# A fused two-block transformer kernel on one core: the loading order and closing norm of the second expert layer, and the order of three steps in the rwkv pair loop

## What is computed

```python
def rwkv_readout(y, q, p):            # first block, each head of 64 columns
    mean = jnp.mean(y, axis=-1, keepdims=True)
    var = jnp.mean(jnp.square(y - mean), axis=-1, keepdims=True)
    yn = ((y - mean) * lax.rsqrt(var + RW_GN_EPS)).reshape(b_, n, RW_DIM) * ln_w + ln_b
    bonus = jnp.einsum('blhn,bldhn,hn->blh', r, k, rk)[..., None] * v
    return (yn + bonus.reshape(b_, n, RW_DIM)) * g

# second block, for every group and expert in it
hg = jnp.einsum('td,edf->tef', xf, w_gate[gi]); hu = jnp.einsum('td,edf->tef', xf, w_up[gi])
act = jax.nn.silu(hg) * hu * comb[:, gi, :, None]
out = out + jnp.einsum('tef,efd->td', act, w_down[gi])
h = h + gate_f * out
return _rms_norm(h, norm_out_w)       # the kernel's result
```

## Time and profile before

| | us |
|---|---|
| median of 3 runs (3620.74 to 3626.2) | 3621.44 |
| the profiled execution | 3619.01 |
| its span in the trace | 3617.2 |
| PE busy, share of the span | 3184.0, 88% |
| DVE busy | 1488.0, 41% |
| ACT busy | 988.5, 27% |
| `route`, from its first transfer to the first instruction of the experts | 3243.97 to 3278.62 |
| experts, to the last down product | 3278.62 to 3581.0 |
| stores, gathers, sums, last norm | 3581.0 to 3617.2 |

### The profile page before, as it was taken

One profiled execution on the slowest core, in us unless ns is written; L12 is line 12 of the kernel. 1 busy time (PEld: TensorE's weight loads), 2 busy tenths in 40 slices (PEclk: granted clock), 3 DMA queues, 4 the chain that ended last, 5 costly groups with the idle time before them and its releaser, 6 DMA issues. The chain is left out here.

```text
span 3617.2 us, 54475 instructions
## 1 busy us (share of the span) xinstructions
PE 3184.0 (88%) x23420; PEld 1762.2 (49%) x23420; DVE 1488.0 (41%) x3058; ACT 988.5 (27%) x1956; POOL 46.7 (1%) x65
## 2 busy tenths in 40 slices
PE   7899999998799999789995987787989999884995
PEld 3566666666655555444442332334455554441432
DVE  3677776877457568510023110103242424331122
ACT  2344344334124655510011000002324243310000
POOL 0000000000000000000000000000000000000001
PEclk9999999999799999889997999998999999986998
DMA  4122222211311222243056999963111011037998
GB/s 174 54 67 65 80 69 83 77 59 50 111 51 64 79 80 69 102 151 116 0 204 281 421 421 421 421 274 157 73 47 73 27 69 47 7 139 295 417 417 328
DMA packets 119456, 555.31 MB, mean 154 GB/s; under 512 B 32320, under 2 KB 35120, under 8 KB 83632
## 3 DMA queue, kind: packets, MB, share of 16 engines
q1 hardware_dynamic: 113072, 532.95, 38.4%
q0 software_dynamic: 3456, 12.58, 0.9%
q10 hardware_dynamic: 2688, 6.29, 0.4%
HBM read 518.03 MB, written 33.74 MB: 153 GB/s over the span
## 5 line engine op out<-in xcount | busy, mean ns | idle before, releaser
L2347 PE MATMUL mh_ps<-mh_w_ahead,xmT 128*128 128x512 f32 x768 | 336.5, 593 | 0.0
L2082 PE MATMUL ex_ps<-ex_ring,ex_xs 128*64 128x512 f32 x896 | 244.9, 636 | 49.8 <-DMA ex_ring<-expert_slabs_in 37.5
L495 PE MATMUL rw_ps<-hT,rw_w 128*128 128x512 f32 (+1 forms) x640 | 255.8, 529 | 7.8 <-PEq L63 5.8
L2347 PEld LDWEIGHTS mh_ps<-mh_w_ahead,xmT 128*128 128x128 f32 x768 | 144.7, 190 | 167.1 <-issue 165.2
L2082 PEld LDWEIGHTS ex_ps<-ex_ring,ex_xs 128*64 128x64 f32 x896 | 82.7, 146 | 201.9 <-issue 199.9
L1273 PE MATMUL sg_ps<-hTp,sg_w 128*128 128x512 f32 x384 | 170.8, 598 | 0.0
L495 PEld LDWEIGHTS rw_ps<-hT,rw_w 128*128 128x128 f32 x640 | 112.1, 191 | 92.4 <-issue 82.8
L2331 PE MATMUL mh_ps<-xmT,mh_w_ahead 128*128 128x512 f32 x256 | 125.0, 622 | 14.8 <-PEq L63 8.5
L2166 DVE TENSOR_TENSOR ex_hid<-ex_hid,ex_ps 128x512 f32<-128x512 f32 x16 | 11.0, 688 | 284.9 <-PE ex_ps L2082 284.9
L1797 PE MATMUL se_ps<-se_w,se_mT 128*128 128x512 f32 x256 | 114.8, 606 | 6.5 <-DMA se_w<-w_out_in 6.5
L2974 PE MATMUL ge_ps<-ge_ring,ge_xs 128*64 128x512 f32 x512 | 116.0, 607 | 2.7 <-DVE ge_xsq L3069 2.7
(11 more groups left out here) (602 smaller groups left out, 5315.1 us busy)
## 6 DMA issues: line engine op xcount, KB each, us to landing
ex_ring<-expert_slabs_in SPq DMA_DIRECT2D x148, 1024.0 KB, 26.8
ge_ring<-expert_slabs_in SPq DMA_DIRECT2D x52, 2048.0 KB, 11.9
mh_w_ahead<-head_slabs_in SPq DMA_DIRECT2D x16, 2048.0 KB, 7.9
rw_mod_w<-mod_w_in SPq DMA_DIRECT2D x64, 384.0 KB, 4.1
ex_first<-expert_slabs_in SPq DMA_DIRECT2D x22, 1024.0 KB, 26.3
rw_mod_w<-ada_in SPq DMA_DIRECT2D x64, 256.0 KB, 3.3
sg_kern<-cum_dram SPq DMA_DIRECT2D x64, 256.0 KB, 3.2
ex_ring<-expert_slabs_in SPq DMA_DIRECT2D x7, 2048.0 KB, 13.8
```

The source lines that it names most:

```text
L495: mm = pe.matmul(where[j, part], w[:, k, P * j:P * j + P], tokens, start=k == 0, stop=k == KC - 1)
L2082: mm = pe.matmul(ps[halves[j], bank, :], src[:, k, halves[j]], home(g + j)[0][:, k, :], start=k == 0, stop=k == KC - 1)
L2347: mm = pe.matmul(ps[:, 4 + t, :], xmT[:, k, P * t:P * t + P], w[:, slot, k, :], start=k == 0, stop=k == KC - 1)
```

## The change

In the rwkv loop: banks 0 and 1 of `near` are swapped, and `near` has one more wait; the bonus product moves ahead of `turn_y`, and so does the first of the three dense steps, which waits for one group of `near` fewer; on ACT `keep_mid(c, 1)` moves ahead of `deviation(c - 1)`. In the second block: `settle` keeps x in SBUF and stores none, and loads the gate and norm rows; `route` loads two slabs and no x; `grouped_experts` loads slabs 2 to 5 of the first pair itself, starts the first gate product one turn earlier, loads two slabs again at the end and not four, lets SP store half of the last quarter rows, and computes and stores the last norm tile by tile, with a root on one element to load ACT's table ahead. `last_residual` is gone.

```diff
-        NEAR = (2, 1, 0)
+        NEAR = (2, 0, 1)
 ...
                 def near(c, d):
                     pe.wait_ge(s.filled, 2 * c + d + 1)
+                    if c:
+                        pe.wait_ge(state_ready[1], 10 * c)
 ...
                         keys(c, 0)
-                        if c:
-                            turn_y(c - 1)
                         pe.wait_ge(s.prepared, c + 1)
                         pe.matmul(ps[:, 3, :], halves, ksum[:, :], start=True, stop=True).then_inc(s.bonus_done, 1)
                     if prep:
                         if p:
                             pe.wait_ge(s.w_in, 16 * p)
                         if core:
+                            pe.wait_ge(s.near_kept, 3 * c + 2)
+                        project_part(1, 0, 0, 1)
+                    if core and c:
+                        turn_y(c - 1)
+                    if prep:
+                        if core:
                             pe.wait_ge(s.near_kept, 3 * c + 3)
-                        project_part(1, 0, 0, 3)
+                        project_part(1, 0, 1, 3)
 ...
                         keep_diag(c, 1)
+                        keep_mid(c, 1)
                         if c:
                             deviation(c - 1)
                         keep_diag(c, 2)
-                        keep_mid(c, 1)
                         keep_mid(c, 2)
 ... settle
-                for t in range(NTT):
+                for t in range(NTT if x_out is not None else 0):
                     sp.wait_ge(s.summed, H * t + H)
                     sp.dma_start(x_out[tile(t), :], x[:, t, :]).then_inc(s.x_stored, 16)
 ... route: with stage(nc, landed.all), and at SP's end
+                sp.wait_ge(landed.rows, rows)
 ... grouped_experts, SP
                     load_rows(0)
                     load_quarters(0)
-                    load_slab(0, 4)
-                    load_slab(0, 5)
+                    for n in range(2, 6):
+                        load_slab(0, n)
                     load_rows(1)
 ...
+                    sp.wait_ge(s.up_used, 2 * NP - 1)
+                    load_slab(0, 0)
+                    load_slab(0, 1)
+                    sp.wait_ge(s.yeq_kept, NP)
+                    for h in range(2):
+                        sp.dma_start(quarter_rows(NP - 1, 1, h), yeq[quarter[2 + h], :]).then_inc(s.yeq_out, 16)
+                    for t in range(NTT):
+                        sp.wait_ge(s.normed, t + 1)
+                        sp.dma_start(x_out[tile(t), :], normed(t)).then_inc(s.x_stored, 16)
+                    sp.wait_ge(s.x_stored, 16 * NTT)
 ... PE
                     turn_rows(0)
-                    turn_quarters(0)
                     for i in range(NP):
                         last = i + 1 == NP
-                        pe.wait_ge(s.xs_kept, turns_before(i + 1, i // 2 + 1))
+                        pe.wait_ge(s.xs_kept, turns_before(i + 1, i // 2 + 1) if i else 1)
 ...
-                            up_quarters(i, n)
+                            if i:
+                                up_quarters(i, n)
+                            elif n == 0:
+                                turn_quarters(0)
+                        if i == 0:
+                            pe.wait_ge(s.xs_kept, 2)
+                            up_quarters(0, 0)
+                            up_quarters(0, 1)
 ... ACT
+                    act.activation(sq[:, 0:1], cst("ones")[:, 0:1], ACT.Sqrt).then_inc(s.squared, 1)
                     for t in range(NTT):
                         act.wait_ge(s.added, t + 1)
-                        if t:
-                            act.wait_ge(s.squared, t)
+                        act.wait_ge(s.squared, t + 1)
                         act.activation(sq[:, :], x[:, t, :], ACT.Square, accum_out=ss[:, t:t + 1]).then_inc(s.squared, 1)
+                        act.wait_ge(s.mean, t + 1)
+                        act.activation(ss[:, t:t + 1], ss[:, t:t + 1], ACT.Sqrt).then_inc(s.root, 1)
 ... DVE
+                    def scale(t):
+                        dve.wait_ge(s.root, t + 1)
+                        link(dve.reciprocal(ss[:, t:t + 1], ss[:, t:t + 1]))
+                        dve.scalar_tensor_tensor(normed(t), x[:, t, :], ss[:, t:t + 1], orow, ALU.mult, ALU.mult).then_inc(s.normed, 1)
 ... behind the two sums of a tile t
                         ins.then_inc(s.added, 1)
+                        if t:
+                            scale(t - 1)
+                        dve.wait_ge(s.squared, t + 2)
+                        dve.tensor_scalar(ss[:, t:t + 1], ss[:, t:t + 1], 1.0 / D, EPS, ALU.mult, ALU.add).then_inc(s.mean, 1)
+                    scale(NTT - 1)
 ... program
+            settle(..., x2, None, ..., xn_keep=xn, x_keep=x, ahead=[gate, norm_out row, four gate pieces])
+            route(..., [(ring[:, n, :], a["expert2_slabs"][n]) for n in range(2)], (landed, 96))
-            last_residual(nc, ss[:, :], orow[:, :], x, out)
```

More of the change, by code:

```diff
@@ L1725, in _, with settle @@
                     dve.tensor_tensor(m[:, t, cols], ga_n, gb_n, ALU.add).then_inc(s.merged, 1)
-def settle(nc, cst, source, rows, norm, x_in, x_out, cols, head, lg, xT=None, xn_dram=None, xn_keep=None, ahead=()):
+def settle(nc, cst, source, rows, norm, x_in, x_out, cols, head, lg, xT=None, xn_dram=None, xn_keep=None, x_keep=None, ahead=()):
     NTT, H, KB = SEQ // P, 2, 8
@@ L1780, in _ @@
                         sp.dma_start(xn_dram[tile(t), :], xn[:, place(t), :]).then_inc(xn_stored[t % 2], 16)
-                sp.wait_ge(s.x_stored, 16 * NTT)
+                if x_out is not None:
+                    sp.wait_ge(s.x_stored, 16 * NTT)
                 if xn_dram is not None:
@@ L1973, in _ @@
                 dve.tensor_copy(lg.rearrange("p t n -> p (t n)"), ps[:, 6, 0:NL * NTT])
[L1976 to L1999, removed]
 CAP = 2 * SEQ // NE
@@ L2767, in first_of_ties, with route @@
         link(dve.tensor_tensor(hot[:, :, e], hot[:, :, e], a, ALU.is_gt))
-def route(nc, cst, raw, bias, weight, slot, npass, ahead):
+def route(nc, cst, raw, bias, weight, slot, npass, ahead, before):
     NTT, G, E = SEQ // P, 4, 4
@@ L2788, in route @@
         ps = keep.enter_context(nc.psum_tensor("rt_ps", [P, 2, 512], F32, allow_name_mangling=True))
-        with stage(nc) as (s, block, _):
+        landed, rows = before
+        with stage(nc, landed.all) as (s, block, _):
             @block.sync
@@ L2898, in grouped_experts, with quarter_rows @@
                 x_in = [s.x_in0, s.x_in1]
+                def quarter_rows(i, b, h):
+                    first = P * NP + 64 * i + 32 * b
+                    return ye_dram[first:first + 32, 512 * h:512 * h + 512]
                 ye_out = [s.ye_out0, s.ye_out1]
@@ L2918, in _ @@
                     load_quarters(0)
-                    load_slab(0, 4)
-                    load_slab(0, 5)
+                    for n in range(2, 6):
+                        load_slab(0, n)
                     load_rows(1)
-                    for i in range(NP):
-                        nxt = (i + 1) % NP
-                        if 1 <= i and i + 1 < NP:
+                    for i in range(NP - 1):
+                        if i:
                             load_rows(i + 1)
-                        if i % 2 == 1 and i + 1 < NP:
+                        if i % 2 == 1:
                             load_quarters((i + 1) // 2)
@@ L3311, in program @@
                 mixer_heads(nc, masks, xmT, tok, a["head_slabs"], a["gdn_taps"], a["ret_decay"], rope, norm_w[:, :], m, w, xe_dram[0:NE * SLOTS, :])
-            settle(nc, cst, (m, a["w_out2"], None, None), (mod2[0:1, 2 * D:3 * D], None), (col_a, col_sh), x2, x3,
-                   (a["norm_ffn"], part(mod2, 0, 4), part(mod2, 0, 3)), (a["route_w"], 20), wide(20), xn_keep=xn)
+            gate_of = lambda lo, hi, n: mod2[0:1, 5 * D + lo:5 * D + hi].broadcast_to([n, hi - lo])
+            rows = [nc.sbuf_tensor(name, shape, F32, side="right") for name, shape in (("x4", [P, 4, D]), ("gate4", [P, D]), ("gate_q", [P, 512]), ("orow4", [P, D]))]
+            x, gate, gate_q, orow = (keep.enter_context(r) for r in rows)
+            landed = Sems(nc, keep)
+            settle(nc, cst, (m, a["w_out2"], None, None), (mod2[0:1, 2 * D:3 * D], None), (col_a, col_sh), x2, None,
+                   (a["norm_ffn"], part(mod2, 0, 4), part(mod2, 0, 3)), (a["route_w"], 20), wide(20), xn_keep=xn, x_keep=x,
+                   ahead=[(gate[:, :], gate_of(0, D, P), landed.rows), (orow[:, :], a["norm_out"].broadcast_to([P, D]), landed.rows)] +
+                         [(gate_q[32 * n:32 * n + 32, :], gate_of(512 * (n % 2), 512 * (n % 2) + 512, 32), landed.rows) for n in range(4)])
         with ExitStack() as moe:
             sb = lambda name, shape: moe.enter_context(nc.sbuf_tensor(name, shape, F32))
-            x, gate, gate_q, orow, ss = sb("x4", [P, 4, D]), sb("gate4", [P, D]), sb("gate_q", [P, 512]), sb("orow4", [P, D]), sb("ss4", [P, 4])
+            ss = sb("ss4", [P, 4])
```

39 lines of the change are left out of this document (20 added, 19 removed).

## The result

The changed kernel takes 3600.86 us (median of 4 runs, 3596.62 to 3602.84), the one before 3622.8 in its 4 runs beside them: ratio 0.9943, 95% interval 0.9931 to 0.9956. It is 22 us faster; 26.9 were forecast. The time lies 6.9 us above the forecast and 0.4 above the range. Of the 6.9 us 4.9 are the gain that is missing, 1.4 come from the median of before (3622.8 and not 3621.4), and 0.5 from rounding 3594.5 to 3594. The profiled execution of after took 3600.97, its span is 3599.3.

A forecast was written before the change was run, and what follows sets the result against it. Transfers were taken to hold `route`, PE to set the experts' pace, and PE to wait for y in rwkv. Terms -18.5, -3.7, -1.8, -1.9 and -1 gave -26.9 from median 3621.4: 3594.5, stated as 3594, range 3585 to 3600.5.

The forecast's parts named there:

- Part 1: Start of the experts: with two slabs in `route` and x kept, DVE and not transfers holds the stage; -18.5 us.
- Part 2: First pair of the experts: first turn to pair 1 takes 42.0 and not 45.7 us; -3.7 us, late slabs costing zero.
- Part 3: End of the kernel: -1.8 us up to the first gather, -1.9 us from there to the end.
- Part 4: rwkv loop: bonus and dense step fill the wait for y, but root and low-rank products start later; -1 us.
- the three cases -1.9, +0.5 and +3: rwkv loop, cost over six pairs in us: clock stays up, falls as before, or falls in all.
- the clock stays up: rwkv loop: the clock does not fall, given the shorter idle times; -1.9 us over six pairs.
- falls as before: rwkv loop: the clock falls in three of the six pairs, as in the kernel before; +0.5 us.
- (b): rwkv moves cost: root's 0.74 us passed on in seven pairs, or clock falls in all; +5 us, 3600; chance 0.15.
- (a): rwkv moves give all they aim at: root not late, low-rank products do not wait; 3585; chance 0.12.
- (c): Experts' start gives half: loop entry was hidden in SP's wait, or slabs hold first pairs; 3603 to 3605; chance 0.06.
- (d): Experts: slower than before, slabs late in every pair because their lead is two; 3630; chance 0.01.
- (e): `route`: something else holds its end, so the change stays within 0.2% of before; chance 0.02.

The follow-up runs named there:

- e1_rwkv_only: The kernel before with only the rwkv part of the change; 3626.03 us against 3621.53, ratio 1.0014.
- e3_root_first: The changed kernel with ACT making the two copies of `keep_mid(c, 1)` behind the root again; 3602.17 us, ratio 0.9945 to before.
- e11_four_slabs: The changed kernel with four slabs loaded in `route` again, x and the gate and norm rows as in the change; 3607.88 us, one run.
- e12_norm_stage: The changed kernel with the closing norm as a stage of its own again; 3597.38 us, one run.
- e9_bonus_alone: e2_second_only with the bonus product alone moved ahead of `turn_y`, no dense step moved; 3590.07 us, ratio 0.9917 to before.
- e2_second_only: The changed kernel with the rwkv loop of before, so only the second block's part of the change; 3596.26 us, ratio 0.9930 to before.
- e6_table_ahead: The changed kernel with a one-element root on ACT ahead of `keep_diag(c, 0)`, loading the table early; 3592.95 us, ratio 0.9928 to before.
- e8_old_table: e2_second_only plus a one-element root on ACT that takes the rwkv loop's table load ahead; 3581.06 us, ratio 0.9890 to before.
- e5_filler: The changed kernel with one unused matmul per turn ahead of the wait for `bonus_kept`; 3587.55 us, ratio 0.9908 to before.
- e4_five_steps: The changed kernel with two more dense steps moved ahead of the low-rank products; 3582.69 us, ratio 0.9896 to before.
- e7_table_five: The changed kernel with both the early table load of e6_table_ahead and the five steps of e4_five_steps; 3575.12 us, ratio 0.9879 to before.

## Why the forecast was wrong by 6.9 us, step by step

**Part 1, right.** -18.5 forecast, 34.65 - 16.0 = -18.6 measured. DVE's work does hold the stage, and the loop entry costs 1.55 us from DVE's last instruction (3268.41 against 3269.96), not the 3 more that I allowed for.

**Part 2, right.** 42.0 forecast from the first turn to pair 1, 41.7 measured. The longest landing that I took as a bound, 17.8 us, was wrong: 22.2 against 22.9 us from release to use. It cost nothing, by a margin of 0.7. That a landing time of one kernel is a bound for another was not mine to assume: the same 2 MB loads took 11.6 us in one kernel and 15.9 in the other, both with the DMA engines at a share of 0.98 or more, so the time depends on what is queued beside them.

**Part 3, right, with one digit to mend.** Stores to gather: 3.86 forecast, 3.15 measured. Gather to end: 27.9 forecast, 27.1 measured, since a tile takes 3.97 us and not 4.3 (two sums, one scaling and two small steps). Together -5.2 us where I had -3.7.

**Part 4, the mechanism right and the size wrong.** The order of the lists gave what was worked out: `turn_y` at T + 3.11 (3.1), the low-rank products at T + 7.60 (7.6), with PE idle ahead of them. The failed step is the price of the clock, in the three cases -1.9, +0.5 and +3. I read it off the start of the low-rank products, T + 8.60 against T + 7.22, and the cases +0.5 and +3 put these products at T + 8.4, that is 0.8 us for a fall. That reading holds for before, where the low stretch (568.8 to 572.2) ends ahead of the products (575.04) and costs 1.3 us. In after it begins behind them: in the second turn they start at T + 7.60, as if there were no fall, and the low stretch runs from 367.3 to 374.1. So its price does not show at that place at all, and it is not 0.8 us but 1.7 for the 3.4 us low stretches and 3.2 for those of 6.8, which the trace of before does not show in these six turns. I also took -1, a value between "the clock stays up" and "falls as before"; it fell in five pairs of six.

For the two profiles the falls cost 3 x 3.2 + 2 x 1.7 = 13.0 us in after and 3 x 1.3 = 3.9 in before, and the later products 6 x 0.38 = 2.3 at most. That makes 11.4, and 10.1 us were between them. But the profile of after is the worst of its kind. Low clock in the five kernels with this order is 27.2, 20.5, 17.1, 20.5 and 20.5 us (after, e1_rwkv_only, e3_root_first, e11_four_slabs, e12_norm_stage), 21.2 in the mean; in the two with the old order it is 10.2 and 20.4, 15.3 in the mean. Half of the difference is 3 us, and with the 2.3 for the later products the part should cost about 5; the runs say 4.5, where I had -1. So some half of the cost is the clock, and half the products that start later. Both sums are estimates from single profiles. By the medians this is the miss: -25.9 - 1 = -26.9 forecast, -25.3 + 4.5 = -20.8 from the two parts.

**The rivals.** (b) was right in its outcome, 3600, and in part in what it said of the clock, which fell in five turns and not in all; its other half, the root passed on, fell with e3_root_first. I gave it 0.15 and had a row for it; I should have asked what a change does that makes the idle time end elsewhere. (a) is refuted for this order, though e9_bonus_alone shows that half of it was to be had. (c), (d) and (e) did not occur.

**What stays open.** Why the clock fell in five pairs and stayed up in one of the same profile (in the other profiles of this order it fell in three or four), and why it is low for 3.4 us here and 6.8 there. The idle time of a turn does not settle it alone: 2.35 us in one piece gave 10.2 and 20.4 us of low clock (before, e2_second_only), 2.36 in three pieces 17.1 to 27.2 (after, e1_rwkv_only, e3_root_first, e11_four_slabs, e12_norm_stage), 2.20 in three pieces 3.4 (e9_bonus_alone), 2.0 in two pieces 17.0 (e6_table_ahead), and 1.52 in one piece and less 0 (e8_old_table, e5_filler, e4_five_steps, e7_table_five). Each is a single profile, and single profiles of one loop differ by 10 us.

## What to carry to other kernels

When work is moved into a wait, add up the idle time of the whole turn before and after: here it was 2.35 and 2.36 us, so nothing was filled, and the clock fell behind what was left. Price a wait of the engine that sets the pace by the clock behind it as well as by its length, and look for that in PEclk and the counts of matmuls, since the busy time doesn't show it. And compare a loop in two profiles only after two profiles of the same code have shown how far they differ.

## What the runs showed that I had not expected

A useless matmul, 1.02 us in the trace, in each of six turns made the kernel 13 us faster. Two profiles of the same loop differed by 10.8 us, with 10.2 and 20.4 us at the low clock. A table load taken out of the path to y, to where ACT waits anyway, was worth 8 us in one order and 15 in another, for 7 loads of 1.28. And a slab took 15.9 us to land where it took 11.6 before, at nearly the same DMA rate (411 and 415 GB/s), with no wait of PE to tell of it.
